# Scores of both heads in one step, second passes of 64 rows in two halves of the array, three score banks

## The reference

```python
# forgetting attention: 8 heads of 64, 512 tokens, query blocks of 128
logit[t, s] = q_t . k_s / sqrt(64) + F[t] - F[s],  s <= t
# sparse attention: 8 heads of 64; an indexer picks 128 keys for each query
logit[t, s] = q_t . k_s / sqrt(64) + bias[bucket(t - s)],  s picked and s <= t
p = softmax(logit);  out = p @ v
```

## Time and profile before

| what | value |
|---|---|
| median of three runs | 1390.11 us |
| the profiled execution | 1390.86 us, span 1389.1 us |
| PE busy | 1361.6 us (98%), mean granted clock 0.991 |
| DVE, ACT, POOL busy | 816.7, 517.7, 562.8 us |
| attention, first score to last | 703.2 to 857.8 us |

### The profile page before, as it was taken

How to read it: one execution, slowest core, us unless ns; L and a number is a source line. 1 busy time by engine, 2 the same in 40 slices (tenths; PEclk the granted TensorE clock), 3 DMA queues, 4 the chain that set the end, 5 groups by cost and what they waited for, 6 DMA issues and landing times.

```text
span 1389.1 us, 18486 instructions
## 1 busy us (share of the span) xinstructions
PE 1361.6 (98%) x6394; PEld 1108.3 (80%) x6398; DVE 816.7 (59%) x1082; ACT 517.7 (37%) x818; POOL 562.8 (41%) x230
## 2 busy tenths in 40 slices
PE   8998999999999999999999999999999999999997
PEld 6787878888888888887777777888878888888886
DVE  5463568484766847885988866334554343352474
ACT  5333234331322314234356665323345323142233
POOL 4323335353562646324322223443524535345361
PEclk9999999999999999989999999999999999999999
DMA  7454235365473754713522233333422423323221
GB/s 222 117 89 98 76 106 159 98 178 157 143 227 99 210 167 112 212 34 106 77 77 63 75 92 83 100 91 91 141 72 93 134 77 109 88 89 119 79 91 60
DMA packets 213252, 156.68 MB, mean 113 GB/s; under 512 B 8996, under 2 KB 193696, under 8 KB 213064
## 3 DMA queue, kind: packets, MB, share of 16 engines
q1 hardware_dynamic: 212728, 154.62, 39.9%
q10 hardware_dynamic: 464, 1.27, 0.3%
HBM read 151.13 MB, written 4.74 MB: 112 GB/s over the span
## 4 chain that ended last, share of the span: by engine, by line
PE 50%; DVE 2%; ACT 1%; issue 0%; POOL 0%; ACTq 0%; DVEq 0%
PE ps L551 28%; PE ps L1020 12%; PE ps L969 3%; PE ps L908 2%; PE ps L885 1%; PE ps L872 1%; PE ps L858 1%; PE ps L859 1%; DVE work L2082 1%; DVE work L2079 0%; DVE work L2064 0%; PE ps L862 0%; DVE top L2062 0%; DVE sel L2067 0%; POOL w_lo L514 0%
## 5 line engine op out<-in xcount | busy, mean ns | idle before, releaser
L514 POOL TENSOR_TENSOR w_lo<-raw,w_hi 128x1024 fp32r<-128x1024 f32 x222 | 559.3, 2527 | 792.9 <-ACT w_hi L1067 792.6
L551 PE MATMUL ps<-u_hi,w_hi 128*128 128x512 f32 x984 | 396.5, 403 | 4.0 <-POOL w_lo L514 2.3
L551 PE MATMUL ps<-u_hi,w_lo 128*128 128x512 f32 x984 | 385.6, 392 | 0.0
L551 PE MATMUL ps<-u_lo,w_hi 128*128 128x512 f32 x984 | 385.4, 392 | 0.0
L1067 ACT ACTIVATE w_hi<-raw 128x1024 fp32r<-128x1024 f32 x222 | 233.0, 1054 | 283.5 <-PE ps L1020 91.0
L551 PEld LDWEIGHTS ps<-u_hi,w_hi 128*128 128x128 f32 x984 | 187.0, 190 | 43.0 <-POOL w_lo L514 4.3
L551 PEld LDWEIGHTS ps<-u_hi,w_lo 128*128 128x128 f32 x984 | 185.9, 189 | 39.9
L551 PEld LDWEIGHTS ps<-u_lo,w_hi 128*128 128x128 f32 x984 | 186.3, 189 | 36.8 <-issue 1.0
L551 PE MATMUL ps<-y_hi,w_hi 128*128 128x512 f32 x320 | 126.7, 396 | 0.1
L551 PE MATMUL ps<-y_hi,w_lo 128*128 128x512 f32 x320 | 124.6, 389 | 0.0
L551 PE MATMUL ps<-y_lo,w_hi 128*128 128x512 f32 x320 | 124.6, 389 | 0.0
(11 more groups left out here) (270 smaller groups left out, 1826.6 us busy)
## 6 DMA issues: line engine op xcount, KB each, us to landing
raw<-w_in SPq DMA_DIRECT2D x69, 512.0 KB, 3.9
raw<-w_mlp SPq DMA_DIRECT2D x64, 512.0 KB, 3.9
adaw<-w_ada SPq DMA_DIRECT2D x32, 768.0 KB, 4.6
raw<-w_up SPq DMA_DIRECT2D x32, 512.0 KB, 5.9
raw<-w_down SPq DMA_DIRECT2D x32, 512.0 KB, 6.6
raw<-w_out SPq DMA_DIRECT2D x16, 512.0 KB, 4.1
bias_rows<-fbrow SPq DMA_DIRECT2D x4, 640.0 KB
xtok<-x SPq DMA_DIRECT2D x4, 512.0 KB, 7.6
```

The lines of the kernel that those rows point to most:

```text
L514: pool.tensor_tensor(w_lo[:, s, :], raw[:, s, :], w_hi[:, s, :], ALU.subtract).then_inc(lo_ready[s], 1)
L551: last = pe.matmul(ps[0:cols, bank, :], w[:, s, c], r[:, k, :], start=(k == ks[0] and w is w_hi and r is r_hi), stop=(k == ks[-1] and w is ...
```

## The change

Both heads' scores of a block are now one call, `s_pair`, made at the even steps: first both first passes, then both second passes, then both masks. The second pass of a head uses only its own 64 rows of `q_dn` and `k_both`, so the two lie in two halves of the array; `q_dn` shrinks from four to two slots and needs no zeros. Scores take turns over three banks (4, 5 and 2). Score `n` waits for the logits of score `n-3`. The first score in bank 2 waits until the value projection has left it.

```diff
+SCORES = (SA, SB, 2)
...
-        q_up, q_dn = sb("q_up", [P, 4, T], F32R, where=merge), sb("q_dn", [P, 4, T], F32R, where=merge)
+        q_up, q_dn = sb("q_up", [P, 4, T], F32R, where=merge), sb("q_dn", [P, 2, T], F32R, where=merge)
...
-            def s_step(p, n):
-                i, hh = n // 2, n % 2
-                if n == 0:
-                    pe.wait_ge(sem("q_ready"), 2 * p + 3)
-                    pe.wait_ge(sem("k_ready"), 2 * p + 2)
-                wait(pe, sem("att_logit"), 8 * p + n - 1)
-                keys = (i + 1) * P
-                bank, at = SA + hh, 2 * (p % 2) + hh
-                q = slice(i * P, (i + 1) * P)
-                pe.matmul(ps[:, bank, 0:keys], q_up[:, at, q], k_both[:, at, 0:keys], start=True, stop=False)
-                pe.matmul(ps[:, bank, 0:keys], q_dn[:, at, q], k_both[:, at, 0:keys], start=False, stop=False)
-                if p >= NQ:
-                    pe.wait_ge(sem("sel_ready"), i + 1)
-                    last = pe.matmul(ps[:, bank, 0:keys], identb[:], sel[:, i, 0:keys], start=False, stop=True)
-                else:
-                    last = pe.matmul(ps[:, bank, keys - P:keys], identb[:], causalb[:], start=False, stop=True)
-                last.then_inc(sem("att_s"), 1)
+            def s_pair(p, i):
+
+                if i == 0:
+                    pe.wait_ge(sem("q_ready"), 2 * p + 2)
+                    pe.wait_ge(sem("k_ready"), 2 * p + 2)
+                if p == 0 and i == 1:
+                    pe.wait_ge(bank_free[2], st_val.turn(2, 1) + 1)
+                keys, q = (i + 1) * P, slice(i * P, (i + 1) * P)
+                n = 8 * p + 2 * i
+                banks = [SCORES[(n + hh) % 3] for hh in range(2)]
+                for hh in range(2):
+                    at = 2 * (p % 2) + hh
+                    wait(pe, sem("att_logit"), n + hh - 2)
+                    pe.matmul(ps[:, banks[hh], 0:keys], q_up[:, at, q], k_both[:, at, 0:keys], start=True, stop=False)
+                for hh in range(2):
+                    at, b = 2 * (p % 2) + hh, slice(hh * HD, (hh + 1) * HD)
+                    pe.matmul(ps[:, banks[hh], 0:keys], q_dn[b, at // 2, q], k_both[b, at, 0:keys], start=False, stop=False)
+                for hh in range(2):
+                    if p >= NQ:
+                        pe.wait_ge(sem("sel_ready"), i + 1)
+                        last = pe.matmul(ps[:, banks[hh], 0:keys], identb[:], sel[:, i, 0:keys], start=False, stop=True)
+                    else:
+                        last = pe.matmul(ps[:, banks[hh], keys - P:keys], identb[:], causalb[:], start=False, stop=True)
+                    last.then_inc(sem("att_s"), 1)
...
-            for n in range(LOOK):
+            for i in range(LOOK // 2):
                 pieces.pop(0)()
-                s_step(0, n)
+                s_pair(0, i)
+                pieces.pop(0)()
...
-                    if coming < 16 * NQ:
-                        s_step(coming // 8, coming % 8)
+                    if coming < 16 * NQ and n % 2 == 0:
+                        s_pair(coming // 8, coming % 8 // 2)
...
-                dve.tensor_tensor_reduce(prob(n), ps[:, SA + n % 2, 0:keys],
+                dve.tensor_tensor_reduce(prob(n), ps[:, SCORES[(8 * p + n) % 3], 0:keys],
...
-            dve.memset(q_dn[HD:P, 0:4:2, :].bitcast(F32), 0.0)
-            dve.memset(q_dn[0:HD, 1:4:2, :].bitcast(F32), 0.0).then_inc(sem("q_ready"), 1)
```

More of the change, by code:

```diff
@@ L2125, in q_lows @@
                 dve.wait_ge(sem("q_hi"), 4 * g + 4)
-                dve.tensor_tensor(q_dn[0:HD, at, :], ps[0:HD, 0, :], q_up[0:HD, at, :], ALU.subtract
+                dve.tensor_tensor(q_dn[0:HD, g % 2, :], ps[0:HD, 0, :], q_up[0:HD, at, :], ALU.subtract
                                   ).then_inc(sem("q_ready"), 1)
-                dve.tensor_tensor(q_dn[HD:P, at + 1, :], ps[HD:P, 0, :], q_up[HD:P, at + 1, :], ALU.subtract
+                dve.tensor_tensor(q_dn[HD:P, g % 2, :], ps[HD:P, 0, :], q_up[HD:P, at + 1, :], ALU.subtract
                                   ).then_inc(sem("q_ready"), 1)
-                dve.wait_ge(sem("q_ready"), 2 * g + 3)
+                dve.wait_ge(sem("q_ready"), 2 * g + 2)
                 dve.sem_inc(bank_free[0], 1)
```

## The result

The changed kernel takes 1391.86 us (median of ten runs, 1390.57 to 1394.39), the kernel before 1389.76 beside it (ten runs, 1386.93 to 1391.52). The ratio is 1.0025, with a 95% interval of 1.0015 to 1.0035: slower by about 3.5 us (2.1 to 4.9), where +2.7 was forecast. The two medians alone differ by 2.10. The runs of one kernel lie up to 5 us apart: in the sets run beside the experiments those of the kernel before under 1387.2 us have a mean granted clock of 0.994 or 0.995, the others 0.991 to 0.993. The profiled execution took 1390.57 us, span 1388.8.

A forecast was written before the change was run, and what follows sets the result against it. PE, busy 98%, was taken as the bound. The terms 3.9 - 0.6 + 0.1 - 0.7 gave +2.7 us, so 1392.8 us for the median, with a range of 1386.5 to 1397.0.

The forecast's parts named there:

- second passes: Attention on PE: pairs' second passes in halves cost 14.3 us in eight groups against 10.4, so 3.9 us more.
- pairing, masks, groups 0 to 3: Mask weight loads on PE: the first of two masks saves 0.04 in each of 16 pairs, 0.6 us.
- group 0's stalls: PE's three stalls in group 0: they stay, end 0.4 to 0.5 later, and add only 0.1 us.
- group 4 and the start of group 5: PE's stall at 800.06: gone, because DVE has about 0.78 more in hand; 0.7 us less.
- Rival 1: Second passes: the halves pay in full, nothing lost in and out; 6.5 us less, 1383.6; chance 12%.
- Rival 2: DVE's early scores: `sel` or logits come one POOL subtraction earlier, all 3.5 us of stalls go; 1389.9; chance 10%.
- That score is now made one step earlier, the wait goes: Groups 1 to 3: DVE's wait of 0.78 for the second score of block 2 goes.
- The zeros: DVE before group 0: two zero writes take 2.3 us; without them DVE waits 2.9 for the first score, worth nothing.
- Rival 3: Starts of groups: DVE loses the race with POOL in groups 1 to 6, about 0.7 each; 1397.0; chance 18%.
- the signs that were to show the forecast right: Paired loads 6 to 10 ns apart, group 0 stalls near 712 or 715 and at 720.9, none at 800, no 0.78 wait.

The follow-up runs named there:

- single_half: Kernel before with each single score's second pass on its own 64 rows, order and two banks as before; 1401.71 us, ratio 1.0099.
- pair_full: Changed kernel with second passes over all 128 rows again and the zeros back, pairs and three banks kept; 1389.55 us, ratio 1.0004.
- single_banks3: Kernel before with three score banks in turn and nothing else; 1390.26 us, ratio 1.0014.
- after_plan_k: Changed kernel with block 2's last three selection rounds one slot earlier on DVE and `k_lows` ahead of the even score's logits; 1389.06 us, ratio 1.0000.
- pair_banks2: Changed kernel with two score banks instead of three, pairs and halves kept; 1397.52 us, ratio 1.0066.
- after_tt: Changed kernel with both heads' transposes ahead of the pair at even steps; 1397.13 us, ratio 1.0066.

## Why the prediction was right, and where not

The sign and the size came out, with luck in the parts: +2.7 was forecast, +3.5 measured. By terms, from the table and the pairs:

| term | forecast | measured |
|---|---|---|
| second passes | +3.9 | +3.6 (0.46 x 8, halves against full passes) |
| pairing, masks, groups 0 to 3 | -0.6 | about -1.0 (0.25 x 4) |
| group 0's stalls | +0.1 | about +0.8 |
| group 4 and the start of group 5 | -0.7 | about -0.4 |
| starts of other groups | 0 | about +0.2 each, 5 times |

1. **Second passes: right.** The switch costs what the indexer's rows showed, 0.10 in, 0.11 of exposed load and 0.10 out. A pair of 384 keys takes 0.37 from load to mask load as worked out. Rival 1, that the halves pay in full, is out: single_half shows 0.24 to 0.28 lost in a visit, and the pair only shares it. The "up to 2x" that the Trainium skill gives ("TensorEngine Tiling (Array Packing)", section "Theoretical Speedup") stands there without a price for the switch, and this case doesn't reach it: against two full passes of 0.36 the two halves take 0.37 at 384 keys, and the way in lies ahead of that.
2. **Masks: right sign, too small.** Two masks and the piece's first matmul take 0.41 from 727.68 to 728.09. Less the piece's 0.23 this is 0.18, against twice 0.13 before: 0.08 saved in this pair, where I had 0.04; were it so for all four sizes, 0.32 a group. By another way: groups 1 to 3 grow by 0.39, which is 0.46 of halves, some 0.2 of stall and so about -0.25 of pairing. A third way is direct: two single scores before against the pair of pair_full, from first pass to the piece's second matmul and with one piece matmul of 0.31 counted once, are 0.02, 0.08, 0.08 and 0.09 longer for the four sizes, 0.27 a group. The three agree within 0.1.
3. **Group 0: the place right, the size wrong.** The collision stayed, as forecast. The step that failed is "I add only 0.1": I took the three stalls as shifted, each with its price. But the score that waited at 712.04 no longer waits, since it has the third bank, and PE goes on to the next thing that hangs on the same DVE chain. The two stalls become one, the clock falls to its lower level for 3.4 us, and together that costs about 0.7 more than I added, although the stall of 720 is gone but for a remainder. single_banks3 shows this by the bank alone (+0.57), pair_full with pairs (+0.78). Rival 2, that all stalls go, did not come; its counter-argument, that the transposes wait for the same chain, is what happened.
4. **Groups 1 to 3: wrong.** "That score is now made one step earlier, the wait goes" names only one of two conditions. The logits also wait for the transposes of step 1, and these come later since the odd score lies ahead. DVE's wait grew from 0.78 to 1.80, it comes some 0.3 later to `k_lows`, and PE waits for it at the first pair of a group. after_plan_k moves `k_lows` alone and takes this away; before the change the same place had 0.12 of wait by PE's starts (transposes at 739.71, first pass at 740.08, 0.37 apart, where after_plan_k shows 0.25 as the least), after it 0.32 (736.95 and 737.52).
5. **Group 5's start: wrong, and partly made good.** The stall's cause, the collision of 789.16 and 789.29, was not touched by the wait. Group 4 is paced by DVE, 20.66 us before and 20.63 after, so its pairs' extra on PE, some 0.35 to 0.45, was hidden in the stall of 0.7. In pair_full, where PE has no extra, group 4 is as long, and the stall is whole. First the changed kernel's first pass there, then that of pair_full:

```profile
798.25 0.41 PE L863 MATMUL ps<-k_both,q_up 128*128 128x128 f32 x2 [0.17 <-issue]
```

```profile
798.74 0.30 PE L863 MATMUL ps<-k_both,q_up 128*128 128x128 f32 x1 [0.62 <-issue]
```

   The forecast's -0.7 was -0.4 for this other reason, so its being near is luck.
6. **The zeros: right in worth.** All of the 2.3 us that they took was given back as idle, but in two places: DVE waits 1.63 for ACT's `q_up` at 691.68, where it did not wait before, and 1.54 for the first score instead of 0.64. The forecast put the whole 2.9 at the first score.
7. **Rival 3: did not come.** POOL's subtraction of 728.62 starts just behind DVE's second normalization in group 1, and no new collision showed in groups 1 to 3. The margin before was 0.03 us, so this one execution does not show that it always holds.

Of the signs that were to show the forecast right, the paired loads and the stall near 715 of before's time came; the stall at 720.9 and DVE without its wait did not, and at the start of group 5 a stall of 0.17 is left. The errors partly cancel: +0.7, +1.0 and +0.3 in steps 3 to 5 against -0.3 in the second passes and -0.4 in the masks. The measured terms add up to +4.0, 0.4 more than the attention grew; a term is read to about 0.1 a group, and the list of terms leaves out what groups 5 to 7 gain by pairing. The sum is nearer than its terms, and that is luck.

## What to carry to other kernels

Cutting a pass in half over rows cost more than it gave here, with one pair of matmuls between a way in and a way out. By these prices it needs more matmuls in the halves per switch, which no run tried: count the switches, not the rows. Before a buffer is added, ask what the waiting engine will stand at next: if it hangs on the same chain, the stalls only join, and a joined stall can cost the clock as well. For every wait that a change should remove, list all semaphores at that instruction, not the one that the trace names as last.

The simplest of the three best versions, which the times don't tell apart, changes neither passes nor banks. It runs three rounds of the selection on DVE one slot earlier, so that one instruction no longer meets POOL's: 1386.61 us, about 0.1% under the kernel before.

## What the runs showed of the hardware that was not expected

- **One long stall against two short.** In group 0, behind idle stretches of 2.06 us (single_banks3), 2.17 (after), 2.46 (pair_full) and 3.12 (pair_banks2), the granted clock was at its lower level for 3.4 us, from 0.5 to 1.4 us after work had begun again. Two idle stretches of 1.19 and 0.58 with 2.1 us of work between them in the kernel before left it at 1.00. In after_tt, where PE stands for 2.20 us and 0.4 us later for another 1.11, the lower clock lasted 6.8 us. Length alone does not decide it: after an idle stretch of 2.11 us at 53.3 us the clock stayed at 1.00 in after, and after one of 2.10 at 52.7 us 3.4 us at the lower level followed in before; 1.74 and 1.73 us near 1030 left it at 1.00 in both. It can fall without a stall as well: from 608.60 to 622.25 us before it was 0.50 with no idle stretch over 0.05 us in the 20 us ahead; the last 2.9 us of these held matmuls of one or two columns. Whether the fall in group 0 comes in every execution, one profile of each kernel doesn't show.
- **A visit to a half of the array** costs 0.24 to 0.28 us over a full pass in single_half, for 128 to 512 columns. About 0.10 of it lies ahead of the load (first to second pass 0.24 instead of 0.13 with 128 columns, 0.41 instead of 0.32 with 512), and the rest is the exposed load and the way back.
- **A stall in one group hides work in it.** Group 4 absorbed all that the halves cost it, since DVE set its length: 20.66 us before and 20.63 after.
